# First MLP matrix by seven products for eight: 28 of its 32 output tiles in 14 pairs, each product 256 columns wide

## The reference, cut to what matters

```
h2 = rms_norm(x, norm2_w) * (1 + scale2) + shift2          # [512, 1024]
ff = jnp.square(jax.nn.relu(h2 @ w_mlp1)) @ w_mlp2         # 1024 -> 4096 -> 1024
x  = x + gate2 * ff
```

## Time and profile before

| | |
|---|---|
| median of 3 runs | 1573.8 us (1573.61 to 1575.58) |
| the profiled execution, first to last instruction (span) | 1574.7 us |
| instructions | 23289 |
| time of the profiled execution outside the span | not given; the span is 0.9 us above the median |
| VectorE busy | 954.1 us (61%) |
| ScalarE busy | 796.5 us (51%) |
| GpSimd busy | 837.1 us (53%) |
| mean granted TensorE clock | 0.997 |

### The profile page before, as it was taken

The page is one execution under the profiler, slowest core; times in us unless marked ns, Lnnn a source line. Parts: engine busy times, 40 slices in busy tenths (PEclk is TensorE's granted clock), DMA queues, the critical chain, the costliest instruction groups (busy, mean ns, idle before and its releaser), DMA issues.

```text
span 1574.7 us, 23289 instructions
## 1 busy us (share of the span) xinstructions
PE 1546.3 (98%) x7911; PEld 1246.6 (79%) x7911; DVE 954.1 (61%) x1366; ACT 796.5 (51%) x1492; POOL 837.1 (53%) x601
## 2 busy tenths in 40 slices
PE   7999999999999999999999999999999999999998
PEld 4778888888778756787778888888888888888887
DVE  4798887888639787588362221212258895467542
ACT  4775676666633687323343232423457665454442
POOL 0556665666656786456745444444553467423314
PEclk9999999999999999999999999999999999999999
DMA  8433434434332210366523333333322334222212
GB/s 322 134 124 125 133 102 128 141 101 128 107 96 65 81 28 1 128 240 243 178 75 100 94 106 95 94 97 96 95 87 80 95 103 119 86 69 64 69 43 81
DMA packets 77477, 171.28 MB, mean 109 GB/s; under 512 B 8320, under 2 KB 10752, under 8 KB 73920
## 3 DMA queue, kind: packets, MB, share of 16 engines
q1 hardware_dynamic: 70064, 133.09, 28.0%
q10 hardware_dynamic: 7312, 36.83, 6.6%
HBM read 167.67 MB, written 2.23 MB: 108 GB/s over the span
## 4 chain that ended last, share of the span: by engine, by line
PE 72%; DVE 10%; issue 7%; POOL 5%; ACT 1%; DMA 1%; ACTq 0%; POOLq 0%; DVEq 0%; SPq 0%
PE bank L1282 11%; PE bank L1284 11%; PE bank L1283 11%; PE bank L1300 8%; PE bank L1303 8%; PE bank L1301 8%; POOL w_lo L642 4%; DVE ada_acc L1986 2%; DVE rstd L2306 2%; PE bank L1632 1%; PE bank L1852 1%; PE bank L1570 1%; DMA w_raw<-ws 1%; PE bank L1643 1%; PE bank L1624 1%
## 5 line engine op out<-in xcount | busy, mean ns | idle before, releaser
L642 POOL TENSOR_TENSOR w_lo<-w_raw,w_hi 128x512 fp32r<-128x512 f32 x455 | 659.3, 1470 | 571.2 <-ACT w_hi L695 570.9
L1282 PE MATMUL bank<-a_hi,w_hi 128*128 128x512 f32 (+1 forms) x1016 | 399.9, 394 | 2.6 <-ACT gates_early L760 1.2
L1284 PE MATMUL bank<-a_hi,w_lo 128*128 128x512 f32 (+1 forms) x1016 | 392.8, 387 | 0.0
L1283 PE MATMUL bank<-a_lo,w_hi 128*128 128x512 f32 (+1 forms) x1016 | 392.3, 386 | 0.0
L695 ACT ACTIVATE w_hi<-w_raw 128x512 fp32r<-128x512 f32 x457 | 263.8, 622 | 158.0 <-PE bank L1303 120.5
L1282 PEld LDWEIGHTS bank<-a_hi,w_hi 128*128 128x128 f32 x1016 | 191.0, 188 | 45.3 <-issue 4.7
L1283 PEld LDWEIGHTS bank<-a_lo,w_hi 128*128 128x128 f32 x1016 | 191.0, 188 | 39.2 <-issue 1.9
L1284 PEld LDWEIGHTS bank<-a_hi,w_lo 128*128 128x128 f32 x1016 | 190.8, 188 | 39.3
L1300 PE MATMUL bank<-b_hi,w_hi 128*128 128x512 f32 x536 | 210.8, 393 | 1.3 <-POOL w_lo L642 1.3
L1303 PE MATMUL bank<-b_lo,w_hi 128*128 128x512 f32 x536 | 209.6, 391 | 0.0
L1301 PE MATMUL bank<-b_hi,w_lo 128*128 128x512 f32 x536 | 209.3, 390 | 0.0
(11 more groups left out here) (404 smaller groups left out, 2607.3 us busy)
## 6 DMA issues: line engine op xcount, KB each, us to landing
w_raw<-ws SPq DMA_DIRECT2D x457, 256.0 KB, 2.7
cs_rows<-cs_scratch ACTq DMA_DIRECT2D x16, 1024.0 KB, 5.3
ada_piece<-ada ACTq DMA_DIRECT2D x16, 1024.0 KB, 5.1
ada_piece<-ada SPq DMA_DIRECT2D x8, 1024.0 KB, 17.7
x_stream<-x SPq DMA_DIRECT2D x2, 1024.0 KB, 7.8
x_stream<-x ACTq DMA_DIRECT2D x1, 2048.0 KB, 8.0
out<-x_stream SPq DMA_DIRECT2D x4, 256.0 KB, 2.2
out<-x_stream SPq DMA_DIRECT2D x8, 128.0 KB, 1.8
```

Of the source, the lines that this page charges most:

```text
L642: nc.gpsimd.tensor_tensor(wlo[b][:, :], raw[n % RAW_RING][:, :], r32(whi[b][:, :]), ALU.subtract)\
L1282: mm(out, lh, rh, start=first, stop=False)
L1283: mm(out, lh, rl, start=False, stop=False)
L1284: return mm(out, ll, rh, start=False, stop=last)
```

## The change

Two output tiles of the first matrix (256 hidden features) and the two halves of the tokens are treated as a 2x2 block product: the weights of a pair are four quarters of 4 blocks each (input blocks even or odd, first or second tile), the input four quarters of 4 blocks by 256 tokens. The product needs eight multiplications of quarters in the usual way. The new scheme (Winograd's form of Strassen's) does seven, with sums of weight quarters and of input quarters as factors:

- The MLP goes in eight parts of 512 hidden features. Part 0 is made by four ordinary tiles ("m1", 0 to 3). The other seven parts are 14 pairs. A pair (i) is 7 products of 4 blocks and 3 matmuls per block, each of 256 columns, into the left halves of banks 3, 4 and 5; then follow 4 ordinary "m2" tiles of 4 blocks (12 matmuls of 512 columns) of the part before.
- Each pair loads 4 slabs as before. Products 0, 4 and 5 use a loaded slab, the other four use a sum of slabs that VectorE makes (`add_weights`, 4 additions of 128x512). All seven have their own `w_hi` and `w_lo`, so that 3 more slabs per pair go through ScalarE and GpSimd.
- h2 is kept in full, and once for all pairs VectorE makes from it four sums per pair of blocks (`first_sums`, `second_sum`, `last_sums_of_inputs`), ScalarE rounds them (`round_inputs`, 8 instructions) and VectorE subtracts (`sums_low`, 8).
- Banks are shared: product 1, then 3, then 5 go on accumulating in bank 4 (DOWN), and TensorE waits before each until VectorE has taken the state of the bank out (`taken`). Product 4 goes on in bank 3 (UP) once ScalarE has kept product 0, and product 6 in bank 5 (ACROSS).
- ScalarE and VectorE make the two hidden tiles from the halves so assembled. `recurrence_rates` moves to the end of part 6. SyncE's and GpSimd's loops over the slabs are written out from the first pair on (SyncE to the end, GpSimd for the pairs). `norm_split` goes; its work is done by a loop that writes `h2`, with the same instructions.

The core of the diff:

```diff
+def product(name, out, moving, first=False, made=None):
+    for j, (b, o) in enumerate(weights(name)):
+        if made is not None:
+            pe.wait_ge(t_ready, ONCE + made + j + 1)
+        both = moving(j)
+        mm(out[:, LEFT], whi[b][:, o:o + P], both[:, 0, :], start=(first and j == 0), stop=False, ...)
+        mm(out[:, LEFT], whi[b][:, o:o + P], both[:, 1, :], start=False, stop=False, ...)
+        ins = mm(out[:, LEFT], wlo[b][:, o:o + P], both[:, 0, :], start=False, stop=(j == BPS - 1), ...)
+    ins.then_inc(gemm_done, 1)
 # TensorE, seven_products(i, e, half)
+    product(names[0], UP, in_h2(0, LEFT), True)
+    product(names[1], DOWN, in_sums(1), True, round0)
+    product(names[2], ACROSS, in_sums(0), True, round0)
+    pe.wait_ge(taken, 3 * i + 1)
+    product(names[3], DOWN, in_sums(2), False, round1)
+    pe.wait_ge(first_copied, ONCE + i + 1)
+    product(names[4], UP, in_h2(1, LEFT))
+    pe.wait_ge(taken, 3 * i + 2)
+    product(names[5], DOWN, in_sums(3), False, round1)
+    pe.wait_ge(taken, 3 * i + 3)
+    product(names[6], ACROSS, in_h2(1, RIGHT))
 # TensorE, the MLP
-for f in range(FQ):
...
+tile_pair((("m1", 0), ("m1", 1)), in_a, in_a_lo, lambda k: (rdyA, KT + k + 1))
+for m in range(2, HIDDEN):
+    feature_tile(("m1", m), in_a, in_a_lo)
+for e in range(EIGHTHS):
+    for half in range(2):
+        if e + 1 < EIGHTHS:
+            seven_products(2 * e + half, e + 1, half)
+        for m in range(half * KT // 2, (half + 1) * KT // 2):
+            feature_tile(("m2", e, m), ...)
 # ScalarE
+hi_upto(slab_of(("m1", 0)) + AHEAD)
+for n in range(KT // 2):
+    round_inputs(n)
+for m in range(2):
+    hi_upto(slab_of(("m1", m)) + AHEAD)
+    hidden_tile(m)
+for i, (e, half) in enumerate(PAIRS_OF_HIDDEN):
+    q0 = slab_of(("sp", e, half, 0))
+    if i == 0:
+        hi_upto(q0 + 2)
+        hi_upto(q0 + 4)
+        hidden_tile(2)
+        round_inputs(KT // 2)
+        round_inputs(KT // 2 + 1)
+        keep_first(i, e, half)
+        round_inputs(KT // 2 + 2)
+        round_inputs(KT // 2 + 3)
+        hi_upto(q0 + 6)
+        hidden_tile(3)
+    else:
+        hi_upto(q0 + 6)
+        keep_first(i, e, half)
+    hi_upto(q0 + 11)
+    hidden_pair(i, e, half)
+    hi_upto(q0 + 16)
 # VectorE
+first_sums()
+second_sum(0)
+for j in range(1, KT // 2):
+    second_sum(j)
+    sums_low(j - 1)
+sums_low(KT // 2 - 1)
+hidden_low(0, 0)
+hidden_low(1, 1)
+add_weights(0, 0)
+add_weights(0, 1)
+for i, (e, half) in enumerate(PAIRS_OF_HIDDEN):
+    if i == 0:
+        last_sums_of_inputs(0)
+        last_sums_of_inputs(1)
+        sums_low(KT // 2)
+        last_sums_of_inputs(2)
+        sums_low(KT // 2 + 1)
+        without_first(i, names[1], t[0])
+        last_sums_of_inputs(3)
+        sums_low(KT // 2 + 2)
+        sums_low(KT // 2 + 3)
+    else:
+        without_first(i, names[1], t[0])
+    without_first(i, names[3], t[1])
+    lower_right(i)
...
+    lower_tile(i, names[5])
+    upper_right(i, names[6])
+    add_weights(i + 1, 0)
+    hidden_low(HIDDEN + 2 * i, hidden_at(e, half, 1))
+    hidden_low(HIDDEN + 2 * i + 1, hidden_at(e, half, 0))
+    for m in range(half * KT // 2, (half + 1) * KT // 2):
+        add_mlp(e - 1, m)
+        if more and m == half * KT // 2:
+            add_weights(i + 1, 1)
 # SyncE: a raw buffer is free when the last slab made from it has its low part
-for s in range(whole, N_SLABS):
-    sp.wait_ge(lo_done, s - RAW_RING + 1)
+for s in range(whole, N_RAW):
+    sp.wait_ge(lo_done, RAW_FREE[s - RAW_RING])
+# per pair of slabs q0 to q0 + 6: RAW_FREE += [q0 + 4, q0 + 4, q0 + 6, q0 + 7]
```

More of the change, by code:

```diff
@@ L106 @@
 RNN_STEPS = rnn_steps()
+QUARTERS = ((0, 0), (0, 1), (1, 1), (1, 0))
+PRODUCTS = (0, "all", "lower", "left", 3, 2, "rest")
+WEIGHT_SUMS = ("lower", "all", "left", "rest")
+PAIRS_OF_HIDDEN = [(e, half) for e in range(1, EIGHTHS) for half in range(2)]
 def plan():
@@ L130, in values_of, with pair_of @@
             tile(("vh", g, c), VHEADS * CKT, advance=(c == NCH - 1))
+    def pair_of(e, half):
+        nonlocal at
+        for i in range(len(PRODUCTS)):
+            tiles[("sp", e, half, i)] = (len(tiles), at, BPS)
+            at += BPS
+        for block in QUARTERS:
+            order.append((("aq", e, half, *block), BPS))
     tile(("dt",), KT)
@@ L423, in build @@
         ADA = bank[7]
+        UP, DOWN, ACROSS = (bank[b] for b in SP_BANKS)
+        lower, upper = sq
+        LEFT, RIGHT = slice(0, HALF_SEQ), slice(HALF_SEQ, SEQ)
         SCALE_ROWS, SCALE_TURNED = bank[3], bank[7]
@@ L646, in _ @@
             folded = range(slab_of(("dt",)), slab_of(("dt",)) + KT // BPS)
-            stops = sorted({0, folded.stop, fill_at, *summed, *turns, *squares, *masked_at, N_SLABS} - {n for n in (*turns, *squares) if n > N_SLABS})
+            mlp = range(slab_of(("sp", *PAIRS_OF_HIDDEN[0], 0)), slab_of(("m2", EIGHTHS - 1, 0)))
+            stops = sorted({0, folded.stop, mlp.start, mlp.stop, fill_at, *summed, *turns, *squares, *masked_at, N_SLABS} - {n for n in (*turns, *squares) if n > N_SLABS})
             for s, end in zip(stops, stops[1:]):
@@ new lines, in keep_first, with hidden_pair @@
+            def keep_first(i, e, half):
+                wait_tile(act, ("sp", e, half, 0))
+                if i:
+                    act.wait_ge(down_made, i)
+                A(first_kept[:, :], UP[:, LEFT], ACT.Copy).then_inc(first_copied, 1)
+            def hidden_pair(i, e, half):
+                for n, (made, done, src, out) in enumerate(((down_made, 0, lower, 1), (up_made, ONCE, upper, 0)), HIDDEN + 2 * i):
+                    act.wait_ge(made, done + i + 1)
+                    act.wait_ge(rdyB, 24 + n - 1)
+                    A(t[2 + n % 2][:, :], src[:, :], ACT.Relu).then_inc(rectified, 1)
+                    act.wait_ge(rectified, n - HIDDEN + 1)
+                    A(bH[:, hidden_at(e, half, out), :], t[2 + n % 2][:, :], ACT.Square).then_inc(hiB, 1)
@@ L1046, in _ @@
+            for m in range(KT):
+                name = ("m2", EIGHTHS - 1, m)
+                hi_upto(slab_of(name) + AHEAD)
+                wait_evac(act, name)
+                A(aH[:, m, :], xF[:, m, :], ACT.Copy, scale=col("na", m)).then_inc(hiA, 1)
+                square("na", m, xF[:, m, :])
             hi_upto(slab_of(("xb", 0)) + AHEAD)
@@ new lines, in sums_low, with add_weights @@
+            def sums_low(n):
+                j, g = n % (KT // 2), n // (KT // 2)
+                ve.wait_ge(t_high, ONCE + n + 1)
+                if g:
+                    ve.wait_ge(t_made, ONCE + n + 1)
+                    v.settle()
+                two = slice(2 * g, 2 * g + 2)
+                V.tensor_tensor(T_split[:, j, two, 1, :], T_full[:, j, two, :], r32(T_split[:, j, two, 0, :]), ALU.subtract)\
+                    .then_inc(t_ready, 1)
+            def add_weights(i, part):
+                n0 = RAW_OF[slab_of(("sp", *PAIRS_OF_HIDDEN[i], 0))]
+                over, under, corner, beside = (raw[(n0 + j) % RAW_RING] for j in range(len(QUARTERS)))
+                below, every, left, rest = w_sum
+                if i and part == 0:
+                    ve.wait_ge(lo_done, slab_of(("sp", *PAIRS_OF_HIDDEN[i - 1], 0)) + len(PRODUCTS))
+                for n in range(n0, n0 + 3) if part == 0 else (n0 + 3,):
+                    ve.wait_ge(w_in[n % RAW_RING], 16 * (n // RAW_RING + 1))
+                if part == 0:
+                    V.tensor_tensor(below[:, :], under[:, :], corner[:, :], ALU.add).then_inc(sums_made, 1)
+                    ve.wait_ge(sums_made, len(WEIGHT_SUMS) * i + 1)
+                    V.tensor_tensor(every[:, :], over[:, :], below[:, :], ALU.add).then_inc(sums_made, 1)
+                    return
+                V.tensor_tensor(left[:, :], over[:, :], under[:, :], ALU.add).then_inc(sums_made, 1)
+                ve.wait_ge(sums_made, len(WEIGHT_SUMS) * i + 2)
+                V.tensor_tensor(rest[:, :], beside[:, :], every[:, :], ALU.add).then_inc(sums_made, 1)
@@ L2497, in _ @@
+            recurrence_rates()
+            for m in range(KT):
+                add_mlp(EIGHTHS - 1, m)
+                if m:
+                    gain_low("na", m - 1, aL, aH, hiA, 2 * KT, rdyA)
             gain_low("na", KT - 1, aL, aH, hiA, 2 * KT, rdyA)
```

269 lines of the change are left out of this document (180 added, 89 removed).

## The result

| | before | after |
|---|---|---|
| median of 20 runs, us | 1573.7 (1571.73 to 1576.38) | 1576.24 (1572.35 to 1581.26) |
| profiled execution: time, span, clock | span 1574.7 | 1574.61, 1572.8, 0.997 |

The ratio is 1.0015, with a 95% interval of 1.0008 to 1.0021. The medians differ by 2.5 us: slower by a little, inside the 0.2% that I called no change. 1574.4 was forecast. Measured a second time, the same kernel had 1575.54 against 1574.1, ratio 1.0008 (0.9998 to 1.0018).

What follows compares the result with a forecast made beforehand. TensorE, by its number of matmuls times the distance between starts, was taken to bound the MLP. -11.1 + 9.2 + 0.5 + 0.6 + 1.0 = +0.2 us on 1573.8, plus a fifth of a clock fall, gave 1574.4 us; range 1567 to 1580.

Steps and rivals of the forecast that it cites:

- gain on TensorE; period of a pair: MLP: 672 matmuls of 512 columns become 1176 of 256, 152.2 to 141.1 us, gaining 11.1; each pair lasts 20.95 us.
- second half of hidden tile 3 waits for `w_lo`: Start, last ordinary tile: slab s7's low part comes at 823.5 us, TensorE wants it at 822.05; stall 1.5 us.
- product 1 waits for `w_lo`: Start, pair 0: the low part of product 1's weights comes at 829.1 us; stall 1.4 us.
- product 3 waits for `without_first`: Pair 0: VectorE's subtraction comes only at 836.95 us, behind sums slowed by GpSimd; stall 4.8 us, the largest.
- low parts within product 3: Pair 0: VectorE's last two sums and low parts, needed for the third and fourth block, end at 839.3; stall 1.3 us.
- first m2 tile: After pair 0's products: hidden tile 3's low part comes at about 847 us against 846.6; 0.5 us.
- pair 1: Its weight sums come late, so `without_first` of product 1 comes at 861.2 us against 860.6; 0.6 us.
- the end: Part 7: GpSimd's sixth sum of squares ends about 25.5 us in, TensorE wants it at 24.5; 1.0 us (0 to 2).
- the clock: Gap of 4.8 us before product 3: a fall would slow about 3.5 us of products, +2 to +3; a fifth put in.
- Rival 1: Start: VectorE and GpSimd contention costs less than thought, the start then costs 3.5 to 5 us; 1567 us, chance 0.19.
- The ring: Steady pairs: SyncE's waits for raw weight buffers make a cycle of 20.4 us, 0.55 below the pair's 20.95; cost 0.
- Rival 3: The clock falls in the gap before product 3 of pair 0, adding 2.5 us; 1576.5 us, chance 0.12.

Runs made afterwards that it cites:

- e4_tail: e1 plus four small matmuls in TensorE's wait ahead of the tail's sums of squares; 1574.26 us, ratio 1.0004 to the kernel before.
- e3: Changed kernel, VectorE's two-SBUF-input operations of the start (except `first_sums`) taking one input from PSUM, not the real operands; 1569.13 us, ratio 0.9958 to the kernel before.
- e7: Changed kernel with the first two raw weight buffers of each pair freed two blocks later; 1596.65 us, ratio 1.0145 to the kernel before.
- e0_after: The changed kernel as it is, run again beside the kernel before; 1575.54 us, ratio 1.0008.
- e2: Changed kernel with ScalarE making the hidden tiles' full squares, VectorE only subtracting; 1574.25 us, ratio 0.9999 to the kernel before.
- e1: Changed kernel with 22 small matmuls before product 3 and 10 before the first m2 tile; 1575.57 us, ratio 1.0007 to the kernel before.

## Why the prediction came out as it did

| step of the prediction | said, us | after, us | at clock 1.00 (e4_tail), us |
|---|---|---|---|
| gain on TensorE; period of a pair | 11.1; 20.95 | 20.97 a pair, no waits | 20.97 |
| second half of hidden tile 3 waits for `w_lo` | 1.5 | 0.8 | 0.8 |
| product 1 waits for `w_lo` | 1.4 | 1.6 | 1.6 |
| product 3 waits for `without_first` | 4.8 | 3.9 | 3.9 |
| low parts within product 3 | 1.3 | hidden in the fall | 1.2 |
| first m2 tile | 0.5 | 2.3 | 2.8 |
| pair 1 | 0.6 | 0 | 0 |
| the end | 1.0 | 0.8 | 0.8 |
| **all holes** (the first four said as 9.2 together) | **11.3** | **9.4** | **11.1** |
| the clock | 0.4 put in, 2 to 3 if it falls | 3.4, in two falls | 0 |
| sum | +0.6 | +1.7 (stretch), +2.5 (medians) | +0.2 (stretch) |

**Right, and shown.** The gain per pair, by the distance of 0.120 us that the earlier trace rows give. The start of pair 0 gives the gain back, by VectorE's queue with GpSimd at work: the addition of 1.03 us to operations that take 0.47 is the 1.05 that the earlier trace rows showed for other sizes, and e3, which removes it, takes 6.7 us off. Rival 1 (little contention) is refuted. By the formula that the Trainium skill (TensorE: Matmul & The Clock Gate, Back-to-back issue gap) gives for the gap of isolated matmuls, a pair would be an estimated 7 x 12 x 0.109 + 48 x 0.216 = 19.5 us. The 20.97 measured speak against it, for these operands. The ring hides; its margin is by the estimate from e7 nearer to 1.1 us than to my 0.55.

**Wrong: the clock.** I gave the fall a chance of 0.12 and put a fifth of it in. It came in both profiles of this kernel, and twice. The step that failed is the reading of the earlier trace rows as something special to the kernel's end; and the 3.5 us of slow products, from which I priced it, stand in no row. Rival 3's fall did come, but not its price of 2.5 us: the fall before product 3 was free, since VectorE set the start of `b_lo`'s matmul with it and without it. What cost 1.5 us is a second fall, behind a hole of 2.1 us, of which I had not thought. That rival 3's 1576.5 lies near 1576.24 is chance. The falls are not a matter of one execution: the median of the runs' mean clocks is 0.995 in the 32 runs of the kernel after, 0.997 in the 29 of the kernel before that were measured beside e0_after, and 0.997 in e4_tail. In the first measurement the runs after spread over 9 us and those before over 5. Falls ahead of the MLP, which are not the change's, are part of that; the rest is open.

**Wrong: the first m2 tile.** I let it want hidden tile 3's low part with its fourth block. The code has one count for all blocks, `lambda k: (rdyB, 24 + HIDDEN * (e + 1))`, so that the third matmul already waits for all four low parts; its start at 841.84 is there in the timeline. I sized the wait by data that it needs and not by the count it is given. By the data alone I should not have been far off: the fourth block's low part would be wanted at 839.07 + 11 x 0.2265 = 841.6, an estimate, and was made at 841.8. No run has the waits one by one. e2, which shortens VectorE's chain, removed the hole.

**Sizes, and luck.** At a clock of 1.00 the holes are 11.1 us where I had said 11.3, and the stretch is +0.2, just my sum without the clock. That is luck in the parts: the first m2 tile was 2.3 us dearer than said, and product 3, hidden tile 3 and pair 1 were 0.9, 0.7 and 0.6 cheaper. The forecast's total then came close because the clock took 1.5 us and not more.

**The tail** cost its 0.8 us, but in the profiled executions it was the tail that decided what an edit at the start was worth: e1, e2 and e3 brought pair 1 forward by 1.6, 3.7 and 8.3 us and lost 1.6, 3.2 and 1.6 of it there. I had no such step.

## What to carry to other kernels

A cheaper product pays only once its operands are ready: price the first turn through the queue of the engine that makes them, and look for an operand in PSUM for whichever VectorE operation runs beside GpSimd (e3 shows what that is worth; no run did it with the real operands). Measure an edit by the distance between two fixed instructions and read the clock in every window of it, since a gain in one place can be lost in the clock of another. Count a wait by its semaphore's number, not by the data behind it, and end a row of clock-keeping matmuls before its hole ends. A fall of the clock costs nothing where another engine sets when TensorE may go on: compare the start of the next instruction that waits, with the fall and without it.
